# A hybrid decoder trunk: the MLP's first trip written out, its first two jobs interleaved by block, the norm's bias additions and a weight split moved

## The reference, cut to what matters

```
x = layer_norm(ALPHA * x + h, W['ln1_g'][i], W['ln1_b'][i])
hid = jax.nn.relu(x @ W['mlp_up'][i])
x = layer_norm(ALPHA * x + (hid * hid) @ W['mlp_down'][i], W['ln2_g'][i], W['ln2_b'][i])
x = x + jax.nn.sigmoid(x @ W['ple_gate'][i]) * (p[i] @ W['ple_proj'][i])
```

## Time and profile before

| | us |
|---|---|
| median of 3 runs | 4293.91 (4286.32 to 4294.7) |
| profiled execution | 4298.19 |
| its span in the trace | 4296.7 |
| TensorE busy with matmuls | 3862.2 (90%) |
| DVE busy | 1624.0 (38%) |
| ScalarE busy | 1167.2 (27%) |
| mean granted clock of TensorE | 0.952 of full speed |

### The profile page before, as it was taken

How to read it: one execution, slowest core, us unless ns; L and a number is a source line. 1 busy time by engine, 2 the same in 40 slices (tenths; PEclk the granted TensorE clock), 3 DMA queues, 4 the chain that set the end, 5 groups by cost and what they waited for, 6 DMA issues and landing times.

```text
span 4296.7 us, 83989 instructions
## 1 busy us (share of the span) xinstructions
PE 3862.2 (90%) x36015; PEld 3386.6 (79%) x36015; DVE 1624.0 (38%) x2134; ACT 1167.2 (27%) x1626; POOL 272.6 (6%) x462
## 2 busy tenths in 40 slices
PE   6979797969899999989699978888878999999989
PEld 4656474758799999979398866676657999999979
DVE  1435353543422232352522165555524323222352
ACT  2232323231412121231122144555432312121131
POOL 2110102020000000000300011111100000000000
PEclk9989898989999999999899999999989999999989
DMA  2222212031111111101122201000011111111112
GB/s 84 63 73 59 76 55 80 22 89 35 35 45 45 45 45 45 45 28 38 26 81 81 85 26 44 26 25 28 25 29 30 40 45 45 42 48 40 45 33 69
DMA packets 312449, 206.08 MB, mean 48 GB/s; under 512 B 26280, under 2 KB 298334, under 8 KB 312094
## 3 DMA queue, kind: packets, MB, share of 16 engines
q1 hardware_dynamic: 299390, 165.58, 13.4%
q0 software_dynamic: 9152, 21.77, 1.8%
q10 hardware_dynamic: 3552, 13.41, 0.8%
HBM read 173.66 MB, written 27.04 MB: 47 GB/s over the span
## 4 chain that ended last, share of the span: by engine, by line
PE 77%; DVE 7%; ACT 4%; issue 4%; SPq 2%; DVEq 1%; PEld 1%; ACTq 1%; PEldq 1%; POOLq 1%; DMA 0%; POOL 0%
PE ps L1668 75%; ACT big L651 2%; SPq L320 1%; PEld ps L1668 1%; SPq L304 1%; DVE xa L1346 1%; ACT xa L651 1%; ACT ring L651 1%; DVE big L1447 1%; DVE h_hi L1089 1%; ACTq L758 1%; DVE big L1258 1%; DVE ring L1089 1%; DVE small L1234 1%; DVE big L1089 1%
## 5 line engine op out<-in xcount | busy, mean ns | idle before, releaser
L1668 PE MATMUL ps<-h_hi,wparts 128*128 128x364 f32 (+1 forms) x4992 | 1002.0, 331 | 38.5 <-DVE h_lo L1342 20.7
L1668 PEld LDWEIGHTS ps<-h_hi,wparts 128*128 128x128 f32 x4992 | 859.6, 189 | 41.3 <-DVE h_lo L1342 22.8
L1668 PE MATMUL ps<-x_lo,wparts 128*128 128x364 f32 (+1 forms) x3360 | 700.0, 333 | 39.2 <-DVE h_hi L1089 39.2
L1668 PE MATMUL ps<-x_hi,wparts 128*128 128x364 f32 (+1 forms) x3072 | 604.5, 331 | 38.8 <-DVE x_lo L1342 21.2
L1668 PEld LDWEIGHTS ps<-x_lo,wparts 128*128 128x128 f32 x3360 | 583.9, 191 | 44.5 <-issue 32.6
L1668 PEld LDWEIGHTS ps<-x_hi,wparts 128*128 128x128 f32 x3072 | 526.7, 189 | 43.3 <-issue 23.7
L1668 PE MATMUL ps<-h_lo,wparts 128*128 128x364 f32 (+1 forms) x2112 | 469.2, 331 | 0.0
L651 ACT ACTIVATE big<-ps 128x512 f32<-128x512 f32 (+10 forms) x334 | 199.8, 621 | 977.1 <-PE ps L1668 438.0
L651 ACT ACTIVATE wparts<-ring 128x1024 fp32r<-128x1024 f32 x200 | 200.5, 1004 | 926.6 <-PE ps L1668 907.4
L1668 PE MATMUL ps<-big 64*64 64x64 f32 (+6 forms) x7192 | 321.8, 265 | 73.3 <-DMA big<-in_cache_v 25.4
L1089 DVE TENSOR_TENSOR wparts<-ring,wparts 128x1024 fp32r<-128x1024 f32 x200 | 232.1, 1160 | 376.6 <-ACT wparts L651 352.0
(11 more groups left out here) (229 smaller groups left out, 3300.3 us busy)
## 6 DMA issues: line engine op xcount, KB each, us to landing
ring<-in_mlp_up SPq DMA_DIRECT2D x64, 512.0 KB, 4.1
ring<-in_mlp_down SPq DMA_DIRECT2D x64, 512.0 KB, 3.9
ring<-in_w_in_even SPq DMA_DIRECT2D x28, 512.0 KB, 7.2
rkv_scratch<-big ACTq DMA_DIRECT2D x24, 544.0 KB, 2.7
big<-rkv_scratch SPq DMA_DIRECT2D x24, 544.0 KB, 4.8
big<-in_cache_k SPq DMA_DIRECT2D x160, 64.0 KB, 1.9
big<-in_cache_v SPq DMA_DIRECT2D x160, 64.0 KB, 1.9
ring<-in_ple_gate SPq DMA_DIRECT2D x16, 512.0 KB, 4.1
```

Of the source, the lines that this page charges most:

```text
L1668: return pe.matmul(out, lhsT, rhs, start=start, stop=stop, skip_group_check=True)
```

## The change

The kernel after differs in five things.

- ScalarE and DVE split unit 1 of the MLP's weights inside the norm ahead of it, right behind unit 0, and no longer in step 1 of trip 0.
- `low(k)` comes one y earlier on DVE: y0 y1 low0 y2 low1 ... y7 low6 low7.
- The 8 bias additions to xa leave the norm (`shifted`). Ahead of the MLP each is made behind the rounding of hidden block t in trip 0; ahead of PLE each is made behind the sigmoid of step t, and DVE waits there for one of them at a time.
- Trip 0 is written out on TensorE, ScalarE and DVE, and the loops go over the rest.
- In trip 0 TensorE makes jobs 0 and 1 together (`dense_pair`): for each block of x nine matmuls of job 0 and nine of job 1, with the two pairs of weight buffers and both halves of PSUM.

```diff
 norm, ScalarE
                 split_w(stage, 0, 0)
+                split_w(stage, 0, 1, 256 if n % 2 else 1024)
                 if n % 2:
-                    split_w(stage, 0, 1, 256)
...
-                for k in range(KT):
-                    act.wait_ge(xlo_ok, split_base(f"norm{n}") + k + 1)
-                    f(xs(xa, k), xs(xa, k), ACT.Identity, bias=par[:, b + k:b + k + 1]).then_inc(ln_done, 1)
+            def shifted(n, b, k):
+
+                act.wait_ge(xlo_ok, split_base(f"norm{n}") + k + 1)
+                f(xs(xa, k), xs(xa, k), ACT.Identity, bias=par[:, b + k:b + k + 1]).then_inc(ln_done, 1)
 mlp, ScalarE
-                            split_w(stage, i, j)
+                            if j > 1 or not first:
+                                split_w(stage, i, j)
...
                             f(xs(h_hi, t), hidden, ACT.Copy).then_inc(hhi_ok, 1)
-
-                with act.Fori(0, 3) as i:
+                            if first:
+                                shifted(2 * layer, 16 + 8 * layer, t)
+
+                trip(0, False, True)
+                with act.Fori(1, 3) as i:
                     trip(i, False)
                 trip(3, True)
...
                     act.drain().then_inc(gate_ok, 1)
+                    shifted(2 * layer + 1, 48 + 8 * layer, t)
 norm, DVE (its splits and its trips change as ScalarE's)
-                    if k >= 2:
-                        low(k - 2)
-                for k in range(KT - 2, KT):
-                    low(k)
+                    if k:
+                        low(k - 1)
+                low(KT - 1)
...
-                    v.wait_ge(ln_done, 16 * layer + 16)
+                    v.wait_ge(ln_done, 16 * layer + 8 + t + 1)
 TensorE
+            def dense_pair(stage, hi, lo, ready):
+
+                jobs = [job(stage, 0, j)[:2] for j in range(2)]
+                for q, used in jobs:
+                    pe.wait_ge(job_free[q], used + 1)
+                pe.wait_ge(wlo_ok, halved(stage, 0, 1) + 1)
+                for k in range(KT):
+                    ready(k)
+                    for j, (q, _) in enumerate(jobs):
+                        for n, (wt, rhs) in enumerate(((w_hi, hi), (w_hi, lo), (w_lo, hi))):
+                            for b, (at, cols) in enumerate(CUTS):
+                                last = mm(bank(3 * q + b, cols), wt[j][:, k * P:(k + 1) * P], xs(rhs, k, at, cols),
+                                          k == 0 and n == 0, k == KT - 1 and n == 2)
+                        if k == KT - 1:
+                            last.then_inc(job_done, 1)
...
+                    if first:
+                        dense_pair(f"mlp{layer}", x_hi, x_lo, normed)
+                    for j in range(2 if first else 0, 2 * KT):
...
+                trip(0, True)
+                with pe.Fori(1, 4) as i:
+                    trip(i)
```

More of the change, by code:

```diff
@@ L840, in mlp, with trip @@
                 stage = f"mlp{layer}"
-                def trip(i, final):
+                def trip(i, final, first=False):
                     for j in range(1, 2 * KT + 1):
                         if j < 2 * KT:
-                            split_w(stage, i, j)
+                            if j > 1 or not first:
+                                split_w(stage, i, j)
                         elif not final:
@@ L1389, in trip @@
                     v.memset(z_scale, 1.0)
-                with v.Fori(0, 3) as i:
+                trip(0, False, True)
+                with v.Fori(1, 3) as i:
                     trip(i, False)
@@ L2021, in mlp, with normed, trip @@
             def mlp(layer):
-                with pe.Fori(0, 4) as i:
-                    def normed(k):
-                        pe.wait_ge(xlo_ok, split_base(f"norm{2 * layer}") + k + 1)
+                def normed(k):
+                    pe.wait_ge(xlo_ok, split_base(f"norm{2 * layer}") + k + 1)
+                def trip(i, first=False):
                     def squared(k):
@@ L2028, in squared @@
                             pe.wait_ge(hlo_ok, i * 9 + (36 * layer + (8 if k == 0 else 9)))
-                    for j in range(2 * KT):
+                    if first:
+                        dense_pair(f"mlp{layer}", x_hi, x_lo, normed)
+                    for j in range(2 if first else 0, 2 * KT):
                         if j < KT:
-                            dense(f"mlp{layer}", i, j, x_hi, x_lo, ready=None if j else normed)
+                            dense(f"mlp{layer}", i, j, x_hi, x_lo)
                         else:
                             dense(f"mlp{layer}", i, j, h_hi, h_lo, ready=squared if j == KT else None)
+                trip(0, True)
+                with pe.Fori(1, 4) as i:
+                    trip(i)
                 norm(2 * layer + 1)
```

## The result

The changed kernel takes 4257.24 us, the median of 4 runs (4254.97 to 4263.36), against 4290.36 us in the median of 4 runs before: a ratio of 0.9923, 95% interval 0.9907 to 0.9939. That is 33.1 us less. The forecast was 21.7 us less, 4272, and the range 4263 to 4286: the direction was right and so were the stages named, the size was not, and the time lies outside the range. The profiled execution went from 4298.19 to 4257.23 us, 41.0 us less.

A forecast was written before the change was run, and what follows sets the result against it. The prediction took TensorE, with 77% of the chain, as the bound, so only its idle time could be saved. Its terms, 2 x (5.0 + 5.5 + 0.35) = 21.7 us, took 4293.91 to 4272.2 us, range 4263 to 4286.

The forecast's parts named there:

- Order of low(k): Norm ahead of the MLP: the first x_lo, and TensorE behind it, start 1.14 us earlier.
- The interleaving and what is late next: MLP trip 0: job 2 stalls 5.8 us, slow restart 2.1 us, job 3 no stall; gain 5.0 us a layer.
- Second weights in norm: Norm ahead of the MLP: the split, 1.04 us on ScalarE and 1.23 on DVE, fits idle holes and costs nothing.
- PLE: First PLE stage: gate 1 starts 3.87 us earlier and 1.6 us of slow restart goes; 5.5 us a layer.
- Trip 0 written out: MLP loop on TensorE: one jump back fewer, 0.35 us gained a layer, bounds 0 and 0.71.
- The rivals: Worse evacuation chain, 4277 to 4282 (0.12); sigmoid table reload, 4283 (0.05); slow instruction supply, 4318 (0.06); no measurable change (0.06).
- The one on written-out trips: TensorE in the MLP: written-out trips are not supplied fast enough, 45 us lost, 4318 us; chance 0.06.
- Scatter: Whole kernel: the runs before spread over 8.4 us, so 4 us were added below the range.

The follow-up runs named there:

- e1_peel: The kernel before with only trip 0 of the MLP written out on TensorE, ScalarE and DVE: ratio 0.9969 (0.9958 to 0.9981).
- e7: The kernel before with TensorE's fourth MLP trip written out in both layers, instead of the first: ratio 0.9963 (0.995 to 0.9977).
- e9: The kernel before with TensorE's fourth MLP trip written out in layer 0 alone: ratio 0.9964 (0.9951 to 0.9977).
- e8: The kernel before with TensorE's fourth MLP trip written out in layer 1 alone: ratio 0.9994 (0.998 to 1.0008).
- e11: The kernel before with 64 drains on TensorE ahead of the first MLP: ratio 1.0 (0.9985 to 1.0015).
- e12: The kernel before with 128 drains on TensorE ahead of the first MLP: ratio 0.9994 (0.9978 to 1.001).

## Why the prediction was wrong

- **Order of low(k)**: 1.14 us forecast, 5.28 - 4.12 = 1.16 us measured. Right.
- **The interleaving and what is late next**: a stall of 5.8 us at job 2 forecast, 5.71 measured; nothing at job 3. The slow restart was 2.8 us in layer 0 and 2.0 in layer 1, where 2.1 were taken. In layer 0, from y0 to job 3's start, it comes to 54.89 - 50.43 = 4.5 us (1140.93 of the kernel before less 0.26 and y0, against 1131.05 less y0), where 5.0 were forecast. Right.
- **Second weights in norm**: no cost seen. From the mean to y0 norm 0 takes 18.1 us instead of 19.8.
- **PLE**: 3.87 + 1.63 forecast, 3.8 + 1.5 measured, twice. Right, the kept clock included.
- **Trip 0 written out**: this step failed. The prediction priced it as one jump, 0.35 us a layer with 0.71 as the bound, and took every stage outside the change as fixed. TensorE's idle time at the jumps of a layer's MLP fell from 2.46 and 2.72 us (three jumps) to 1.35 and 1.34 us (two), 1.1 and 1.4 us; with 4.5 us that gives 5.6 and 5.9 of the MLP's 6.7 and 5.4 us. So the forecast of 5.3 us came out near by two small errors that offset each other, 0.5 us too much for the interleaving and 0.8 too little for the jump. In e1_peel the idle time fell likewise and the MLP was no shorter. What the term missed lies elsewhere: a trip of TensorE written out in layer 0 is worth 13, 16 and 15 us by the ratios of e1, e7 and e9, nearly all of it outside the MLP, and nothing that can be told in layer 1 (e8). In e7 and e9 the mean granted clock rises with it (0.958 against 0.955); in e1 it hardly does. With some 14 us in the place of the 0.7 for the jumps the sum is 21.0 + 14 = 35 us; measured were 33.1 and 36.5. The 14 us come from the kernel before with this part alone; the changed kernel without it was not measured.
- **The rivals**: none came true. The one on written-out trips looked for a loss in their own matmuls, not for a gain elsewhere.
- **Scatter**: I took 4 us of scatter from three runs. Over 86 runs the kernel before lies between 4271 and 4308 us.

Why a written-out trip in layer 0 is worth more than its jump stays open, and so does the stage in which the time is won. That it is no scatter of the runs is shown by the intervals of e1, e7 and e9, which lie clear of 1. That it is won in the RWKV-7 stretch is not shown: kernels that keep their loops have that stretch as short. Placing of the code is not ruled out either. It shows in the stages of e11 and e12, with no net effect, and other amounts were not tried. The kernel with only layer 1 written out is slower in the RWKV-7 stretch than all others (1172 to 1178 us), though its code ahead of the stretch is the same, and makes no difference in total. I have no account of that.

## What to carry to other kernels

Ask of a stage that waits block by block what its end leaves behind it: two jobs that end together want both their evacuations at once, and the next job's weights must be ready before, not after, these. A stop of TensorE costs its own length and, if it is long, a slow restart: 0.66 and 1.11 us cost nothing more here, 5.7 us cost 2.8 in one layer and 2.0 in the other. When TensorE's stream is restructured, forecast the untouched stages with an allowance for the granted clock, and compare the mean clock of many runs before crediting the edit. Before a gain of 10 us is placed in a stage, compare that stage in every profile at hand, those of kernels that lack the edit above all: here three profiles against three looked clear, and three more, of kernels that keep their loops, undid it.

## What was not expected of the hardware

- Writing out one of TensorE's four trips in layer 0 took 13 to 16 us off some 4291 (e1, e7, e9), where the jump had cost 0.7 to 1.1 us. The same in layer 1 alone took nothing that can be told (ratio 0.9994). The cause is open.
- Moving TensorE's code by 64 or 128 drains put a second stop of 0.8 to 1.3 us behind each jump back, in the MLP of one layer and not in the other (one profile each).
- The time of executions of the same kernel follows the mean granted clock: over 86 runs (4271 to 4308 us) time and (1 - clock) x time correlate at 0.93.
- The same stop of 6.2 us is followed by a restart that costs anything from 1.5 to 2.9 us, by the profile and the layer.
